# One hybrid decoder layer on one core: in the last block, sums of squares behind the tiles, three interleaved groups, six groups in accumulator banks, evacuation one pair ahead

## What is computed

```python
def rmsnorm(x, g):
    y = xf * lax.rsqrt(jnp.mean(xf * xf, axis=-1, keepdims=True) + EPS)
    return (y * g).astype(x.dtype)

# trunk_layer(x, p, ...)
mix = jnp.concatenate([a, hm], axis=-1) @ w_out      # conv branch and mLSTM branch
x = x + rmsnorm(mix, g_mix_post)
up = rmsnorm(x, g_ffn_pre) @ w_up                    # 1024 -> 5632
up, ffn_buf_new = causal_dwconv(up, ffn_buf, w_conv_ffn, b_conv_ffn)   # width 3
f = jax.nn.gelu(up[..., :D_FF], approximate=True) * up[..., D_FF:]
x = x + rmsnorm(f @ w_down, g_ffn_post)
x = x + (p @ w_ple) * jax.nn.sigmoid(rmsnorm(x, g_ple) @ w_ple_gate)
```

## Time and profile before

| | us |
|---|---|
| three runs | 2742.85, 2739.90, 2739.43 |
| their median | 2739.90 |
| the profiled execution | 2740.0 |
| its span, first to last instruction | 2738.2 |
| PE busy within the span | 2696.9 (98%) |
| DVE busy | 1706.0 (62%) |
| ACT busy | 919.5 (34%) |
| POOL busy | 242.1 (9%) |

### The profile page before, as it was taken

How to read it: one execution, slowest core, us unless ns; L and a number is a source line. 1 busy time by engine, 2 the same in 40 slices (tenths; PEclk the granted TensorE clock), 3 DMA queues, 4 the chain that set the end, 5 groups by cost and what they waited for, 6 DMA issues and landing times.

```text
span 2738.2 us, 37969 instructions
## 1 busy us (share of the span) xinstructions
PE 2696.9 (98%) x14687; PEld 2602.5 (95%) x14687; DVE 1706.0 (62%) x3688; ACT 919.5 (34%) x1944; POOL 242.1 (9%) x180
## 2 busy tenths in 40 slices
PE   9989999999999999999999999999999999899998
PEld 7979999999999999999999999999999998799998
DVE  6975798865656665555666663746866546472644
ACT  5354434453532122443321233532112425211113
POOL 4422625321000000000000000000000000000000
PEclk9999999999999999999999999999999999999999
DMA  9747989878466666565666666556666584466665
GB/s 325 290 147 295 345 324 371 326 268 315 178 225 232 232 232 232 209 253 199 230 218 243 231 230 246 199 216 228 232 234 232 202 280 141 175 233 232 234 230 190
DMA packets 125118, 660.61 MB, mean 241 GB/s; under 512 B 22010, under 2 KB 22654, under 8 KB 55182
## 3 DMA queue, kind: packets, MB, share of 16 engines
q1 hardware_dynamic: 111150, 628.29, 62.9%
q10 hardware_dynamic: 13792, 29.92, 3.2%
HBM read 533.04 MB, written 125.11 MB: 240 GB/s over the span
## 4 chain that ended last, share of the span: by engine, by line
PE 93%; DVE 4%; ACT 1%; issue 1%; DMA 0%; POOLq 0%; SPq 0%; POOL 0%; DVEq 0%; ACTq 0%
PE proj L645 29%; PE proj L646 28%; PE proj L647 28%; PE m L828 1%; PE m L683 1%; PE m L857 1%; PE m L822 1%; PE m L858 1%; PE m L839 0%; PE m L645 0%; PE m L646 0%; PE m L647 0%; PE m L773 0%; DVE mix_room L1631 0%; PE m L704 0%
## 5 line engine op out<-in xcount | busy, mean ns | idle before, releaser
L645 PE MATMUL proj<-h_split,w_split 128*128 128x416 f32 x2720 | 975.5, 359 | 9.0 <-DVE h_split L1712 3.1
L646 PE MATMUL proj<-h_split,w_split 128*128 128x416 f32 x2720 | 952.3, 350 | 0.0
L647 PE MATMUL proj<-h_split,w_split 128*128 128x416 f32 x2720 | 947.2, 348 | 0.0
L645 PE MATMUL proj<-f_split,w_split 128*128 128x416 f32 x1568 | 561.4, 358 | 10.2 <-DVE f_split L1712 3.6
L646 PE MATMUL proj<-f_split,w_split 128*128 128x416 f32 x1568 | 550.0, 351 | 0.0
L647 PE MATMUL proj<-f_split,w_split 128*128 128x416 f32 x1568 | 546.8, 349 | 0.0
L645 PEld LDWEIGHTS proj<-h_split,w_split 128*128 128x128 f32 x2720 | 510.0, 187 | 20.8 <-issue 6.4
L647 PEld LDWEIGHTS proj<-h_split,w_split 128*128 128x128 f32 x2720 | 511.0, 188 | 9.8
L646 PEld LDWEIGHTS proj<-h_split,w_split 128*128 128x128 f32 x2720 | 511.4, 188 | 3.0 <-issue 1.0
L645 PEld LDWEIGHTS proj<-f_split,w_split 128*128 128x128 f32 x1568 | 294.7, 188 | 26.6 <-DVE f_split L1933 5.7
L1755 DVE SCALAR_TENSOR_TENSOR cv<-a_ext,vecs,cv 128x416 f32<-128x416 f32 (+1 forms) x480 | 304.2, 680 | 0.0
(11 more groups left out here) (284 smaller groups left out, 2215.6 us busy)
## 6 DMA issues: line engine op xcount, KB each, us to landing
w_split<-w_kept SPq DMA_DIRECT2D x432, 1024.0 KB, 4.8
w_kept<-w_split SPq DMA_DIRECT2D x108, 1024.0 KB, 6.6
w_raw<-in_w_units SPq DMA_DIRECT2D x216, 256.0 KB, 4.6
x_resid<-in_x ACTq DMA_DIRECT2D x5, 1664.0 KB, 12.8
out_y<-x_resid ACTq DMA_DIRECT2D x8, 832.0 KB, 9.2
rows<-in_x ACTq DMA_DIRECT2D x4, 832.0 KB, 8.4
w_raw<-in_x ACTq DMA_DIRECT2D x3, 832.0 KB, 12.1
qkv<-in_p ACTq DMA_DIRECT2D x5, 416.0 KB, 5.2
```

What stands on the lines that cost most here:

```text
L645: mm(dst, w_hi, a_hi, start=first, stop=False)
L646: mm(dst, w_hi, a_lo, start=False, stop=False)
L647: return mm(dst, w_lo, a_hi, start=False, stop=last)
```

## The change

All of it is in the last block.

- **Sums behind the tiles.** `add_residual_last` no longer sums a square after each tile; all seven sums stand behind the last low part. ACT squares tiles 0 to 3 between its high parts as before, and tiles 4 to 7 behind the last one.
- **Third group in the turn.** `two_groups` takes `third`: from the turn's step `third` on, the third group follows with its own tiles from 0. It is 1 in the first norm and 4 in the second. `total_of` and `spread_of` move from the third group (before tiles 3 and 6) to the fourth (before tiles 2 and 5).
- **Six groups in banks.** `extra` also puts the fifth and sixth group into m0 and m2. The seventh and eighth then wait for the first and second (`g - 4`). `facc_of` turns the order of the accumulator banks round in the last block, so that pair 0 does not convolve into m0 and m2.
- **Evacuation a pair ahead.** Up to `UP_AHEAD = 3`, `conv_ffn(j)` evacuates pair j + 1 before it convolves pair j: pairs 0 and 1 stand before convolution 0, pair 2 before convolution 1, pair 3 before convolution 2; convolution 3 has none before it, and pair 4 stands before convolution 4.
- **The last state update earlier.** PE's `decode_state(H - 1)` (six matmuls) moves from behind the eight output groups to behind the fourth; DVE's `state_add(H - 1)` moves from behind the first norm's tiles to between the sums of the mixer's squares.
- **Fewer filler matmuls.** `warm(m5, 14)` becomes `warm(m5, 10)`.

```diff
@@ -240,6 +240,9 @@
 TURN_ENDS = (8, 14, 24, 31, 37, 47, 54)
 assert [k for c, k in TAPS_FIRST if c == DIAGONAL] == list(range(PRODUCTS_FROM)) and len(TAPS_FIRST) == TURN_ENDS[-1]
 
+
+
+UP_AHEAD = 3
 
 
 BATCHES = ((0, 1, 2, 3), (4, 5, 6), (7,))
@@ -390,7 +393,12 @@
         proj = [ctx.enter_context(nc.psum_tensor(f"proj{i}", [P, 512], F32)) for i in range(2)]
         m0, m1, m2, m3, m4, m5 = (ctx.enter_context(nc.psum_tensor(f"m{i}", [P, 512], F32)) for i in range(6))
         facc = ((m0, m2), (m1, m5), (m3, m4))
-        extra = {AT[True].g_upa + 2: m5, AT[True].g_upa + 3: m1, AT[True].g_fin + KD + 2: m5, AT[True].g_fin + KD + 3: m1}
+        extra = {first + n: bank for first in (AT[True].g_upa, AT[True].g_fin + KD)
+                 for n, bank in ((2, m5), (3, m1), (4, m0), (5, m2))}
+
+        def facc_of(j, last):
+
+            return facc[2 - j % 3 if last else j % 3]
 
         def bank_of(g, last):
 
@@ -650,7 +658,7 @@
 
                     blocks = blocks_of(g, last)
                     if (part is None or part[0] == 0) and not (last and g in extra):
-                        pe.wait_ge(s_evac.sem, s_evac.free(blk, g - 2 if last and g - 2 in extra else g))
+                        pe.wait_ge(s_evac.sem, s_evac.free(blk, g - 4 if last and g - 2 in extra else g))
                     seen = None if part is None or part[0] == 0 else blocks[part[0] - 1][0]
                     for n in range(*(part or (0, len(blocks)))):
                         u, b = blocks[n]
@@ -714,12 +722,15 @@
                         if then and k in then:
                             then[k]()
 
-            def two_groups(blk, last, g, act, ready):
-
-
-                for n in range(KD):
-                    group(blk, last, g, act, ready, (n, n + 1))
-                    group(blk, last, g + 1, act, None, (n, n + 1))
+            def two_groups(blk, last, g, act, ready, third=None):
+
+
+                for n in range(KD if third is None else KD + third):
+                    if n < KD:
+                        group(blk, last, g, act, ready, (n, n + 1))
+                        group(blk, last, g + 1, act, None, (n, n + 1))
+                    if third is not None and n >= third:
+                        group(blk, last, g + 2, act, None, (n - third, n - third + 1))
 
             for _ in range(8):
                 mm(m0[:, 0:T], stack[:, 0:P], stack[:, :], start=True, stop=True)
@@ -953,12 +964,13 @@
                     elif first and i == 3:
                         then = {2: lambda: norm_spread(blk, n_next, bank=m2)}
                     group(blk, last, out_at(i, mid), f, wait_mix if i == 0 else None, (KD - 1, KD) if i < 2 else None, then)
+                    if last and i == 3:
+                        decode_state(H - 1)
 
                 if last:
-                    decode_state(H - 1)
                     norm_total_last(blk, n_mix)
                     norm_spread(blk, n_mix)
-                    warm(m5, 14)
+                    warm(m5, 10)
                 else:
                     then = {0: {3: total_of(n_mix), 5: spread_of(n_mix)}, 4: {4: total_of(n_ffn)}, 5: {1: spread_of(n_ffn)}}
                     if mid:
@@ -969,11 +981,10 @@
 
                 for half, (up, down) in enumerate(((at.g_upa, at.g_dna), (at.g_upb, at.g_dnb))):
                     if half == 0:
-                        two_groups(blk, last, up, h, wait_h(m_ffn))
+                        two_groups(blk, last, up, h, wait_h(m_ffn), 1 if last else None)
                         if last:
-                            group(blk, last, up + 2, h, then={2: total_of(n_ffn), 5: spread_of(n_ffn)})
                             pe.wait_ge(s_cnew.sem, H)
-                            group(blk, last, up + 3, h)
+                            group(blk, last, up + 3, h, then={1: total_of(n_ffn), 4: spread_of(n_ffn)})
                     for g in range(up + ((4 if last else 2) if half == 0 else 0), up + 2 * FH):
                         group(blk, last, g, h)
                     def wait_f(n):
@@ -1003,10 +1014,10 @@
                         elif i == 2 and last:
                             norm_spread(blk, n_post)
                     elif i == 0:
-                        two_groups(blk, last, at.g_fin + n, f, wait_h(m_ple))
-                    elif i == 2 and last:
-                        group(blk, last, at.g_fin + n, f, then={2: total_of(n_ple), 5: spread_of(n_ple)})
-                    elif i > 1:
+                        two_groups(blk, last, at.g_fin + n, f, wait_h(m_ple), 4 if last else None)
+                    elif i == 3 and last:
+                        group(blk, last, at.g_fin + n, f, then={1: total_of(n_ple), 4: spread_of(n_ple)})
+                    elif i > (2 if last else 1):
                         group(blk, last, at.g_fin + n, f)
 
             for blk in range(NBLK):
@@ -1364,6 +1375,9 @@
                         square(blk, n, i, x[:, i, :])
                     for i in range(done, KD):
                         last_high(i, gain, dst, first)
+                        if i < 4:
+                            square(blk, n, i, x[:, i, :])
+                    for i in range(4, KD):
                         square(blk, n, i, x[:, i, :])
 
                 def table(func, at):
@@ -1430,11 +1444,11 @@
                 def gelu(j):
                     act.wait_ge(s_fext.sem, s_fext.done(blk, j + 1))
                     wide = 432 if last else T
-                    fn(gelu_out[:, j % 3, 0:wide], facc[j % 3][0][:, 0:wide], ACT.Gelu_apprx_tanh).then_inc(s_fgelu.sem, 1)
+                    fn(gelu_out[:, j % 3, 0:wide], facc_of(j, last)[0][:, 0:wide], ACT.Gelu_apprx_tanh).then_inc(s_fgelu.sem, 1)
 
                 def high_f(j):
                     act.wait_ge(s_ff.sem, s_ff.done(blk, j + 1))
-                    fn(f[:, j % FH, 0, :], facc[j % 3][1][:, 0:T], ACT.Copy).then_inc(s_fhi.sem, 1)
+                    fn(f[:, j % FH, 0, :], facc_of(j, last)[1][:, 0:T], ACT.Copy).then_inc(s_fhi.sem, 1)
 
                 for half, (up, down) in enumerate(((at.g_upa, at.g_dna), (at.g_upb, at.g_dnb))):
                     first = half * FH
@@ -1712,7 +1726,7 @@
                             v.scalar_tensor_tensor(dst[:, i - 2, 1, :], x[:, i - 2, :], col(low_gain, i - 2),
                                                    dst[:, i - 2, 0, :].bitcast(F32), ALU.mult,
                                                    ALU.subtract).then_inc(s_h.sem, 1)
-                            sum_squares(n_after, [i - 2])
+                    sum_squares(n_after, range(KD))
 
                 def glu(c, lst, nth):
 
@@ -2157,8 +2171,13 @@
 
                     decayed = state_decay(H - 1)
                     dve.wait_ge(s_cout[0].sem, 16)
-                if last or mid:
-                    sum_squares(n_mix, range(KD - 1 if last else KD))
+                if last:
+                    sum_squares(n_mix, range(4))
+                    after(decayed)
+                    state_add(H - 1)
+                    sum_squares(n_mix, range(4, KD - 1))
+                elif mid:
+                    sum_squares(n_mix, range(KD))
                 else:
                     sum_squares(n_next, range(KD))
                     inverse_root(n_next)
@@ -2171,8 +2190,6 @@
                 dve.wait_ge(s_x.sem, s_x.done(blk, 1))
                 if last:
                     add_residual_last(n_mix, "g_mix_post", n_ffn, m_ffn, "g_ffn_pre", h)
-                    after(decayed)
-                    state_add(H - 1)
                     inverse_root(n_ffn)
                 else:
                     add_residual(n_mix, "g_mix_post", n_ffn)
@@ -2209,10 +2226,12 @@
                 def conv_ffn(j):
 
                     wide = 432 if last else T
-                    s, acc = ext[:, j % 2], facc[j % 3]
+                    s, acc = ext[:, j % 2], facc_of(j, last)
                     g = at.g_upa + 2 * j if j < FH else at.g_upb + 2 * (j - FH)
-                    if last:
+                    if last and (j == 0 or j > UP_AHEAD):
                         up_last(j, g)
+                    if last and j < UP_AHEAD:
+                        up_last(j + 1, g + 2)
                     dve.wait_ge(s_evac.sem, s_evac.done(blk, g + 2))
                     marks = [None, None]
                     for k in range(3):
@@ -2238,7 +2257,7 @@
                         v.tensor_copy(up_tail[:, j, :, :], s[:, :, T:T + 2]).then_inc(s_fconv.sem, 1)
 
                 def gated(j):
-                    val, gate = gelu_out[:, j % 3], facc[j % 3][1]
+                    val, gate = gelu_out[:, j % 3], facc_of(j, last)[1]
                     dve.wait_ge(s_fgelu.sem, s_fgelu.done(blk, j + 1))
                     if last:
                         val_dec, gate_dec = (a[:, TP:432].rearrange("p (b r) -> p b r", r=2 + DEC_S)[:, :, 2:]
@@ -2251,7 +2270,7 @@
 
                 def low_f(j):
                     dve.wait_ge(s_fhi.sem, s_fhi.done(blk, j + 1))
```

(2 more changed lines are left out.)

## The result

| | before | changed kernel |
|---|---|---|
| median of 20 runs | 2739.90 us | 2745.77 us |
| lowest and highest | 2737.97 to 2745.97 | 2741.59 to 2752.26 |
| profiled execution | 2740.0 | 2746.06 |
| its span | 2738.2 | 2744.3 |

The ratio is 1.0021, 95% interval [1.0014, 1.0028]: the changed kernel is 5.9 us slower, 3.2 us above the forecast of 2742.6 and in the stated range (2737.0 to 2747.5). But 5.9 us is more than the 5.5 us (0.2%) that I had called no change, and the interval leaves out 1: "no change that can be measured" did not come true. I had given slower by over 0.2% a chance of 0.16.

What follows compares the result with a forecast made beforehand. PE was taken as the bound, ending last for 93% of the span. 2740.0 + 1.6 (first norm with pairs) + 2.8 (clock) - 1.8 (second norm) = 2742.6 us, range 2737.0 to 2747.5.

Steps and rivals of the forecast that it cites:

- no change that can be measured: Whole kernel: 2742.6 us against 2740.0 before, inside a bound of 0.2%, 5.5 us; chance of within 0.78.
- the crowded loads: Rival, both norms: the fourth group's weights land 1.9 to 3.6 us later, twice; 2746.4 to 2749.8 us, chance 0.14.
- The tiles: First norm: tiles each 1.62 us, PE without gaps, third up group done at 2386.1, about 5.5 us in hand.
- The weight unit takes their place: Before the fourth group PE waits for its weight load: 3.4 us in the first norm, 1.5 in the second.
- The order of the pairs: Two convolutions in a row on DVE make PE idle 4.6 us at the eleventh up group.
- The clock: PE's clock falls at the waits of 3.4 and 4.6 us, costing 1.4 us each, 2.8 us together.
- An idle of 1.5 us is under the 1.80 after which the clock held: Second norm: no clock cost was taken for the 1.5 us weight wait, since the clock held around 1.80 us.
- Fillers at nothing: Ahead of the first norm's tiles: four of 14 fillers go, 1.2 us, worth 0 since tile 1 waits anyway.
- The second norm: PE ends at 2731.4 instead of 2733.2: 1.8 us won, with a weight wait of 1.5 us.
- weights arrive in time: Rival: the fourth group's load costs nothing, so it starts 3.4 and 1.5 us earlier; 2736.3 us, chance 0.08.

Runs made afterwards that it cites:

- The first experiment: The changed kernel with the third up group out of the first norm's turn, following whole: 2739.08 us, ratio 0.9995.
- the one on both turns: The changed kernel with the third group out of the turn in both norms: 2738.61 us, ratio 0.9995.
- The kernel in which the places of low clock are covered and the wait for weights is left in: The changed kernel with UP_AHEAD = 10, 14 fillers ahead of the tiles and 17 fillers ahead of the fourth up group: 2737.21 us, ratio 0.9990.
- the faster version: The changed kernel with UP_AHEAD = 10, 14 fillers, no third group in either turn, total and spread earlier: 2734.49 us, ratio 0.9982.

## Why the prediction was right, and what it mis-sized

- **No change that can be measured**: wrong by a little, since 5.9 us is clear of noise and over the 5.5 us named. The path was as forecast and the clock's term was mis-sized. That the time still lies in the range is in part luck: the range reached up to 2747.5 for a rival, the crowded loads, which did not occur.
- **The tiles**: right. Waits for low parts fell to 0.6 and 0.7 us; in the second norm three of 0.2 us remain, at tiles 2 to 4, where I had named none beyond tile 2. The third up group ended at 2385.5 in a trace that starts the first norm 0.6 us earlier; 2386.1 was worked out.
- **The weight unit takes their place**: right, in place and size. 3.25 us against 3.4, and 1.51 against 1.5. The first experiment shows that it goes with the third group, and the one on both turns that the same holds in the second norm.
- **The order of the pairs**: right. 4.25 us of idle against 4.6, behind DVE's wait for the eighth group. UP_AHEAD = 10 removes it.
- **The clock**: the mis-sized term. I took 1.4 us for each of two waits, at most 1.7, from one low stretch of 3.3 us. In the trace after the low stretches cover 9.5 and 5.3 us of PE's work. At half of it, an estimate, they cost 4.8 and 2.7 us, 7.5 us instead of 2.8. These 4.7 us explain the difference between the worked-out loss of the first part (1.6 + 2.8 = 4.4) and the measured 8.4, and are 0.7 more than it. The bound of 1.7 was wrong too, and the trace of before could have told: it has a low stretch of 6.6 us at its start, over a total and a spread:

```profile
13.40:20.00 6.60, 6.03 (x18) 4.17 (x19) 4.83 (x8) 3.06 (x7) 2.95 (x2) 0.50 0.32 102
```

The profiled execution agrees with the median (2746.06 and 2745.77), but the runs spread by 10.7 us, against 8.0 before, as they would if the low stretches differ from run to run; they do in the traces of the kernels above (10 us, 3.4 us and none behind the same wait), and two of these have low stretches in an earlier block, at 568 and 643 us, that no other trace has.

- **"An idle of 1.5 us is under the 1.80 after which the clock held"**: it came true in the changed kernel, by luck in part, and as a rule it is wrong. In the second norm with UP_AHEAD = 10 the clock fell behind 1.6 us; with the sums alone moved it fell behind 1.8 and 1.2 us; and it held behind 3.2 us with the later total and behind 3.3 us at the ninth group with UP_AHEAD = 0.
- **Fillers at nothing**: doubtful. In five of the eight traces with ten fillers PE stood idle for 0.9 to 1.9 us ahead of tile 0 and the clock was low in the tiles, which I had priced at 0 since the tiles wait for DVE anyway. The idle time did not bring the low clock on in three of them: it had set in among the fillers, before PE began to wait. In the other two the ten fillers ran at the upper level and took 1.9 us, PE then waited 1.9 us, and the clock fell behind that. Of the six traces with 14 fillers (the kernel before included) none shows a low clock in the tiles: in five the low stretch had ended within the fillers, and the sixth has none, with a wait of 1.2 us. The medians differ by 0.9 us, less than their spread, so the price is open.
- **The second norm**: right, 1.7 us won against 1.8.
- **The rival "weights arrive in time"** (2736.3) did not come about: the load landed 4.8 us after its issue, with PE waiting for it. The kernel in which the places of low clock are covered and the wait for weights is left in came to 2737.2, 2.7 us above the faster version (2.2 by the ratios, whose intervals overlap). In the traces the two parts differ by 1.4 and 1.3 us. These kernels differ in the third group, the place of the totals and the 17 fillers together, so how much of it is the wait for weights alone is not shown. The rest of what the first experiment won back goes with the clock: no low stretch at the weights, and a shorter one at the evacuation wait.

## What to carry to other kernels

Before another group is interleaved into a stretch that waits for its input, count the slots of its weights: with three slots, the group behind the turn starts one load after the first group ends, whatever is done in between. An edit that joins many short waits into one long one at equal idle time can still lose, because the clock behind the long one is at stake; let the range reach to the longest low stretch that the trace shows anywhere, and beyond it, not to the nearest one. And where evacuations are moved ahead of the work of a slower engine, look for the place at which the order goes back to normal: there two pieces of that work stand in a row.

## What the runs showed that I had not expected

- The low clock behind one and the same wait for weights (3.2 to 3.3 us) lasted 10.2 us in the traces of the changed kernel and of three variants, 3.4 in one with the sums between the tiles, and did not come at all in the one with a later total. Total and spread were issued within the long ones. The one of 3.4 us set in 1.7 us after the wait had ended, behind the total. Which of wait, place and small matmuls sets the length is open.
- Behind the evacuation wait of 4.0 to 4.2 us the low stretch was 6.8 us long in four traces (the changed kernel among them) and 3.4 in three.
- The granted clock fell behind waits of 1.2, 1.6 and 1.8 us in single traces, and held behind waits of 1.8 us (kernel before), 3.2 and 3.3 us in others.
- Three loads issued within 1.7 us landed 4.8, 6.7 and 8.0 us after their issue in the changed kernel: one behind another, the first not slowed by the others. My rival of crowded loads did not occur.
